# One core: the last twelve experts' weights fetched in order of use, first scan steps prepared among the convolutions, bias product behind K

## What is computed

```
u = rms_norm(h, norm_mix_g)
q, k, v, z, xbc, dt_raw, gate_logits = split(u @ w_in)
y_attn = sliding_window_attention(q, k, v, sinks, rel_bias)      # T5 bias by distance
xbc = silu(causal_depthwise_conv(xbc, conv_w, conv_b))           # 24 tiles of 128 channels
y_ssm = chunked scan over 128 positions, 4 groups of 8 heads      # 2 chunks, then gated norm
merged = gate0 * (y_attn @ w_attn_br) + gate1 * (y_ssm @ w_ssm_br)
h = h + merged @ w_out
logits = rms_norm(h) @ w_router + b_router;  top 4 of 32 experts, softmax weights
for e in range(32):  h += weight_e * ((swiglu(u @ w1[e] + b1[e])) @ w2[e] + b2[e])
out = rms_norm(h, norm_final_g)[16:]
```

## Time and profile before

| | |
|---|---|
| median of three runs | 1416.4 us |
| the profiled execution, its own time | 1421.5 us |
| its span, first to last instruction | 1419.3 us |
| PE busy, share of the span | 93% |
| DVE, ACT, POOL busy | 28%, 19%, 3% |
| chain that ended last | PE 51%, DMA 44%, ACT 2%, DVE 2% |
| DMA rate in the expert stage | 429 GB/s |
| TensorE clock, mean granted | 0.975 |

### The profile page before, as it was taken

The page is one execution under the profiler, slowest core; times in us unless marked ns, Lnnn a source line. Parts: engine busy times, 40 slices in busy tenths (PEclk is TensorE's granted clock), DMA queues, the critical chain, the costliest instruction groups (busy, mean ns, idle before and its releaser), DMA issues.

```text
span 1419.3 us, 18777 instructions
## 1 busy us (share of the span) xinstructions
PE 1315.8 (93%) x7431; PEld 677.6 (48%) x7431; DVE 391.7 (28%) x942; ACT 272.3 (19%) x629; POOL 44.0 (3%) x48
## 2 busy tenths in 40 slices
PE   9999999799999999998899989998899988999897
PEld 5677787455887534343333433333333333333332
DVE  1055466578213432121111211112111121112112
ACT  2124333456200311111111111111111111111111
POOL 3000100031000000000000000000000000000000
PEclk8999999899999999999999999999999999999999
DMA  9533433234875599999999999999999999999993
GB/s 324 155 120 107 131 122 127 104 113 129 285 252 222 208 412 429 429 429 429 429 429 429 429 429 429 429 429 429 429 429 429 429 429 429 429 429 429 429 375 161
DMA packets 73870, 468.49 MB, mean 330 GB/s; under 512 B 4867, under 2 KB 37915, under 8 KB 49228
## 3 DMA queue, kind: packets, MB, share of 16 engines
q1 hardware_dynamic: 70444, 457.89, 79.6%
q0 software_dynamic: 1952, 5.61, 1.4%
q10 hardware_dynamic: 1440, 4.52, 0.9%
HBM read 466.61 MB, written 1.13 MB: 330 GB/s over the span
## 4 chain that ended last, share of the span: by engine, by line
PE 51%; DMA 44%; ACT 2%; DVE 2%; issue 1%; POOL 0%; SPq 0%; DVEq 0%; ACTq 0%; POOLq 0%
PE bank L1271 49%; DMA ring<-in_w 43%; PE bank L1312 0%; DMA rows<-in_g_ssm 0%; PE bank L1381 0%; DVE ring L970 0%; ACT arena L728 0%; ACT arena L642 0%; PE bank L1556 0%; DVE arena L1104 0%; PE bank L1383 0%; PE bank L1665 0%; DVE arena L933 0%; ACT wdt L811 0%; PE bank L1450 0%
## 5 line engine op out<-in xcount | busy, mean ns | idle before, releaser
L1271 PE MATMUL bank<-ring,arena 128*64 128x512 f32 (+3 forms) x2296 | 577.1, 611 | 76.3 <-DMA ring<-in_w 70.3
L1271 PEld LDWEIGHTS bank<-ring,arena 128*64 128x64 f32 (+2 forms) x2296 | 202.4, 146 | 406.6 <-issue 338.7
L1271 PE MATMUL bank<-arena 128*128 128x64 bf16 (+7 forms) x3048 | 358.2, 356 | 7.8 <-ACT arena L709 4.7
L1271 PEld LDWEIGHTS bank<-arena 128*128 128x128 bf16 (+4 forms) x3048 | 177.1, 121 | 210.4 <-issue 195.4
L1271 PE MATMUL bank<-arena,ring 128*128 128x256 f32 (+2 forms) x1312 | 270.0, 386 | 2.5 <-ACT decays L634 1.6
L1271 PEld LDWEIGHTS bank<-arena,ring 128*128 128x128 f32 (+1 forms) x1312 | 217.4, 181 | 45.3 <-ACT decays L634 1.8
L1185 DVE TENSOR_SCALAR arena<-bank 128x256 f32<-128x256 f32 x64 | 27.1, 423 | 697.4 <-PE bank L1271 697.4
L816 ACT ACTIVATE arena<-arena 128x256 f32<-128x256 f32 x64 | 26.7, 417 | 395.1 <-DVE arena L1185 395.1
L823 ACT ACTIVATE arena<-bank 128x512 f32<-128x512 f32 x32 | 19.1, 597 | 310.4 <-PE bank L1271 310.4
L1271 PE MATMUL bank<-arena,wdt 64*128 64x512 f32 (+1 forms) x280 | 69.4, 602 | 0.7 <-ACT arena L823 0.7
L816 ACT ACT_TABLE_LOAD x32 | 41.1, 1283 | 0.6
(11 more groups left out here) (235 smaller groups left out, 584.6 us busy)
## 6 DMA issues: line engine op xcount, KB each, us to landing
ring<-in_w SPq DMA_DIRECT2D x128, 2048.0 KB, 25.4
arena<-in_w SPq DMA_DIRECT2D x64, 2048.0 KB, 29.2
ring<-in_w_in SPq DMA_DIRECT2D x34, 1024.0 KB, 5.4
ring<-in_w_ssm SPq DMA_DIRECT2D x8, 1024.0 KB, 7.9
arena<-cum_rows ACTq DMA_DIRECT2D x8, 512.0 KB, 4.3
ring<-in_w_att SPq DMA_DIRECT2D x16, 256.0 KB, 6.9
ring<-in_w_out SPq DMA_DIRECT2D x4, 1024.0 KB, 4.8
arena<-bias_rows POOLq DMA_DIRECT2D x1, 2048.0 KB, 11.1
```

What stands on the lines that cost most here:

```text
L1271: return tn.matmul(o, lhsT, rhs, start=first, stop=last, skip_group_check=True)
```

## The change

Four edits. (1) From expert 20 on SP issues an expert's six parts in the order in which PE uses them; at the turn, two parts of expert 21 go ahead of expert 20's parts 4 and 5. (2) `ssd_exp` of the first two steps moves to iterations 14 and 18, `ssd_cb` to 14 and 15 (both in bank 7), `ssd_pre` to 17 and 21. (3) The first states go to banks 6, 6, 1 and 5, the first z tile to bank 0, and the last group's `state0` and `st0_save` behind the first scan step. (4) The bias product moves behind the K projection, its eviction behind K's; one more warm-up product stands in each of the two places.

```
-            return bank[it % 2 if it else 3]
+            return bank[it % 2]
+        st0_bank = [bank[6], bank[6], bank[1], bank[5]]
-            return bank[4 + it % 2 if it else 7]
+            return bank[4 + it % 2 if it > 1 else 7][:, P * (it == 1):P * (it == 1) + P]
...
-            def last_two(used):
...
+            TURN = 20
+            def in_order_of_use(used):
+                half = DOUBLED.stop // 2
+                doubled(expert_sources(TURN + 1), (TURN + 1) % 2, used, range(half))
+                single(expert_sources(TURN), TURN % 2, used)
+                doubled(expert_sources(TURN + 1), (TURN + 1) % 2, used, range(half, DOUBLED.stop))
+                single(expert_sources(TURN + 1), (TURN + 1) % 2, used + PARTS)
+                for e in range(TURN + 2, E):
+                    doubled(expert_sources(e), e % 2, used + PARTS * (e - TURN - 1))
+                    single(expert_sources(e), e % 2, used + PARTS * (e - TURN))
...
@@ ACT, convolution loop and scan
+                if i in (14, 18):
+                    ssd_exp((i - 14) // 4)
-                if i in (26, 27):
-                    ssd_exp(i - 26)
-                if i - 5 >= 11 and (i - 5 - 8) % 4 == 3:
+                if i - 5 >= 11 and (i - 5 - 8) % 4 == 3 and i < 28:
                     st0_save((i - 5 - 8) // 4)
             for it in range(8):
+                if it == 0:
+                    st0_save(3)
@@ DVE, convolution loop
+                if i in (17, 21):
+                    ssd_pre((i - 17) // 4)
-            for it in range(2):
-                ssd_pre(it)
@@ PE
-            keep_busy(5)
+            keep_busy(6)
...
-            keep_busy(1)
+            keep_busy(2)
...
             for j in range(2):
                 project(T_K + j, ckv, ...)
+            bias_table()
...
-                if i == 25:
-                    ssd_cb(0)
-                if i - 5 >= 11 and (i - 5 - 8) % 4 == 3:
+                if i in (14, 15):
+                    ssd_cb(i - 14)
+                if i - 5 >= 11 and (i - 5 - 8) % 4 == 3 and i < 28:
                     state0((i - 5 - 8) // 4)
...
             for it in range(8):
                 ssd_y(it)
                 if it + 1 < 8:
+                    if it == 0:
+                        pe.wait_ge(tr_saved, 20)
+                        pe.wait_ge(st0_saved, 3)
                     if it + 2 < 8:
                         ssd_cb(it + 2)
                     z_tile(it + 1)
+                    if it == 0:
+                        state0(3)
```

More of the change, by code:

```diff
@@ L446, in first_experts, with doubled @@
                     fetch(i, sources[1][i], 1)
-            def doubled(sources, odd, used):
-                for i in DOUBLED:
+            def doubled(sources, odd, used, parts=DOUBLED):
+                for i in parts:
                     sp.wait_ge(slot_used, used + (i + 1))
@@ L465, in step @@
                 single(sources, odd, used)
-            def last_two(used):
[L469 to L472, removed]
+            TURN = 20
[8 more added lines that the diff above has]
+                    single(expert_sources(e), e % 2, used + PARTS * (e - TURN))
             first_experts()
             PAIR = 2 * PARTS
-            with sp.Fori(0, E // 2 - 2) as pair:
+            with sp.Fori(0, TURN // 2 - 1) as pair:
                 step(pair * 2 + 1, 1, pair * PAIR)
                 step(pair * 2 + 2, 0, pair * PAIR + PARTS)
-            step(E - 3, 1, (E - 4) * PARTS)
-            last_two((E - 3) * PARTS)
+            step(TURN - 1, 1, (TURN - 2) * PARTS)
+            in_order_of_use((TURN - 1) * PARTS)
             sp.wait_ge(flag_ready, 1)
@@ L485, in _ @@
                     doubled(expert_sources(0), 0, b * (E * PARTS) + (E - 2) * PARTS)
[L486 removed]
+                    with sp.Fori(0, TURN // 2) as pair:
                         step(pair * 2, 0, b * (E * PARTS) + (pair * PAIR + (E - 1) * PARTS))
                         step(pair * 2 + 1, 1, b * (E * PARTS) + (pair * PAIR + E * PARTS))
[L489 to L491 removed]
+                    in_order_of_use(b * (E * PARTS) + (E + TURN - 1) * PARTS)
                 sp.wait_ge(slot_used, PASSES * E * PARTS - PARTS + 1)
@@ L615, in _ @@
                 saved(sc.activation(kT[:, j, :], b[:, 0:NT], ACT.Copy))
+            act.wait_ge(avec_ready, 1)
+            ch.link(sc.activation(avec[0:HEADS, 0, :], bank[5][0:HEADS, 0:VL], ACT.Copy))
+            sc.activation(avec[0:HEADS, 1, :], bank[6][0:HEADS, 0:VL], ACT.Copy).then_inc(avec_saved, 1)
             act.wait_ge(pads_set, 1)
@@ L708, in st0_save @@
                 act.wait_ge(st0_ready, g + 1)
-                sc.activation(hst[:, g, :], bank[6][:, :], ACT.Copy).then_inc(st0_saved, 1)
+                sc.activation(hst[:, g, :], st0_bank[g][:, :], ACT.Copy).then_inc(st0_saved, 1)
             def z_evict(it):
@@ L993, in xdecay0 @@
                                      sc_(decays[0:META, 1, 0, 8 * g:8 * g + 8]), ALU.mult), xdec0_ready, g + 1)
[L995 to L1002, removed]
             def heads(v_, h0=0):
@@ L1019, in ssd_pre @@
                 done(v.tensor_tensor(em[:, it % 2, :, :], em[:, it % 2, :, :],
-                                     cb_bank(it)[:, 0:BLK].unsqueeze(1).to_broadcast([P, HPG, BLK]), ALU.mult), m_ready, it + 1)
+                                     cb_bank(it).unsqueeze(1).to_broadcast([P, HPG, BLK]), ALU.mult), m_ready, it + 1)
+            dve.wait_ge(decay_ready, 1)
+            for i in range(24 + 5):
+                if i < 24:
+                    conv(i)
+                if 0 <= i - 1 < 24:
+                    silu(i - 1)
+                if i - 4 >= 11 and (i - 4 - 8) % 4 == 3:
+                    xdecay0((i - 4 - 8) // 4)
+                if i in (17, 21):
+                    ssd_pre((i - 17) // 4)
             def group_scale(half):
```

26 lines of the change are left out of this document (13 added, 13 removed).

## The result

The changed kernel takes 1402.56 us, median of four runs (1400.53 to 1405.31), against 1416.2 for the kernel before in the same series (1415.23 to 1416.95). The ratio is 0.99 with a 95% interval of 0.9885 to 0.9914. So it is faster, by 13.6 us, and not by 23.6; its time lies just above the range of 1387 to 1401. The profiled execution took 1401.74 us.

A forecast was written before the change was run, and what follows sets the result against it. Weight transfer was taken to pace the experts from the fifth on, PE the end and nearly all before the experts. 10.5 + 8.2 + 4.9 = 23.6 us off gave 1392.8 for the runs, range 1387 to 1401.

The forecast's parts named there:

- Experts: Expert loads in order of use: 7.4 + 3.3 less a hole of 0 to 1.5; 10.5 us gained, range 8 to 12.
- Waits ahead of parts 2 and 3: Expert stage: PE's new waits for parts 2 and 3, put at 1.4 us each.
- a hole of about 1 at the turn: Turn to the new load order at experts 20 and 21: queue runs dry for 0 to 1.5 us.
- an end 5.6 to 7.1 behind the last landing: Last expert: PE ends 5.6 us after the last load lands, instead of 13.0.
- Scan and convolutions: Scan's start: second step 12.5 us earlier, less 4.3 of added loop work; net 8.2, range 2 to 10.5.
- The loop took on: Convolution loop: added work costs 2.0 + 1.6 + 0.5 + 0.2 = 4.3 us, from 2 to 11.
- Start: Kernel's start: with the clock held, K and the bias product end at 23.5 against 28.47; gain 4.9 us.
- I subtract the sum from both: Whole kernel: 23.6 us taken from the profiled 1421.5 and from the median of the runs, 5.1 lower.
- the transposes take 4.3 at full clock in every trace, not 2.7: Start: the 24 transposes would take about 2.7 us with the clock held.
- the idle moment of 0.88 that the sixth warm-up product was to cover: Start: PE's idle moment before the clock's fall, to be covered by a sixth warm-up product so the clock holds.
- The listed sign for being wrong: Start: a half clock in the first 20 us would show the prediction wrong.
- The clock falls at the start: Rival at the start: the clock falls despite the added wide product; 1392.8 + 6.0 = 1398.8, chance 0.2.

The follow-up runs named there:

- before-again: The kernel before, unchanged, profiled once more: 1417.22 us, ratio 1.0003; its profiled execution took 1417.01 with a span of 1414.9.
- e5: Edits 1 to 3 with the start of before, against the kernel before: 1402.13 us, ratio 0.9894.
- e9: e5 with products on constants in PE's waits at the first convolution and iterations 15 and 19: 1398.11 us, ratio 0.9874 against the kernel before.
- e10: e5 with ssd_exp moved to iterations 16 and 20 and ssd_pre to 20 and 24: 1396.04 us, ratio 0.9851 against the kernel before.
- e12: e10 with products on constants also filling the first convolution's wait: 1395.8 us, ratio 0.9858 against the kernel before.
- e2: Only the order of the expert loads from expert 20 on, on the kernel before: 1406.88 us, ratio 0.9927.
- e4: Only the start edit (bias product behind K, two more warm-up products), on the kernel before: 1420.21 us, ratio 1.0022.
- e7: The kernel before with a sixth product in the first warm-up and nothing else: 1417.8 us, ratio 1.0009.
- e3: Only the scan and convolution edits (2 and 3), the scan-only kernel, on the kernel before: 1408.69 us, ratio 0.9951.
- e6: The kernel before with the bias product and its eviction behind K, no added warm-up product: 1418.36 us, ratio 1.001.
- e8: e5 with both ssd_exp at iteration 14: 1405.93 us, ratio 0.9928 against the kernel before.
- e11: e4 with two products on constants in the wait at the first convolution: 1419.19 us, ratio 1.001 against the kernel before.

## Why the prediction was half right

**Experts: right.** 10.5 expected; 9.6 alone, and 10.1 to 10.4 in the traces between the second scan step and the end (before-again 1414.9 - 292.24, changed kernel 1399.9 - 287.37, e5, e9, e10 and e12 likewise). Only e2's own trace, the slowest of its five executions, shows less: 8.3 (1406.4 - 292.05 = 1114.4 against before-again's 1122.7). Waits ahead of parts 2 and 3, a hole of about 1 at the turn, and an end 5.6 to 7.1 behind the last landing were much as put.

**Scan and convolutions: right in sum and in mechanism.** 8.2 expected, 8.3 in the trace, 7.8 in the times. The loop took on 4.05 (4.3 expected): the first scan step of the scan-only kernel starts at 272.53, and without the loop's cost it would be 272.49 less the 4.01 by which the first trace ran late (282.87 in the earlier trace rows against 278.86 in before-again). Of it 2.55 had arisen by iteration 15 (231.08 against 228.53) and 1.49 more by iteration 19 (250.97 against 246.93); nothing came behind that. Expected were 2.0 and 1.6, and 0.7 for `ssd_pre` and the masks. The next activation started 0.01 to 0.02 us behind each of the four added table loads, and taking two of them out did not make the kernel faster. The Trainium skill ("ScalarE: Activation LUTs", What ACT_TABLE_LOAD costs) has a drain of some 1.38 us with every switch. The traces disagree. What the prediction didn't have is that these longer waits of 3.5 and 2.4 can bring the clock down, 4.3 us in the trace of e5.

**Start: wrong, and this is the step that failed.** +4.9 was expected, -3.7 measured, 8.6 of the 10 us that are missing. The step is the sentence "I subtract the sum from both". The 4.9 consisted of the half clock between 12.5 and 22.7 in the one profiled execution, whose time stood 5.1 above the other runs. That number was in the text, and was treated as an offset; it was the very loss that the term wins back. The median had never paid it. Of the other 1.4 us 0.9 are the experts' (9.6) and 0.4 the scan's (7.8). Had the start been worked out for an execution without the fall, the term would have been zero at best: a product moved behind K costs the same there, and two products are added to PE, which waits for little at that place. Smaller errors stand beside it: the transposes take 4.3 at full clock in every trace, not 2.7; and the idle moment of 0.88 that the sixth warm-up product was to cover stood behind ten warm-up passes of 6.10, while in before-again they took 7.24 and left no gap. With a sixth product the next work began 0.9 later in e4 (10.48 against 9.61), and no later in e7 (9.62). The listed sign for being wrong, a half clock in the first 20 us, did not appear; the clock held, and the gain was absent all the same.

**The rivals.** "The clock falls at the start" gave 1398.8 and did not occur: full clock, yet slower than that. The right rival would have been "the clock did not fall before, either".

**Where the 15.0 us between the traces of before-again and of the changed kernel come from:** start -1.87 (24.27 to 26.14), fall at the first convolution -1.5 (5.36 against 3.83), scan +8.3, experts +10.1. The medians differ by 13.6; two of the four runs of the changed kernel lie at 1403.4 and 1405.3, where the falls seen in e5 would put them. That was not traced, and stays open. Single executions 4 to 5 us above their median also stand in e3 (two of six), e6, e8, e9 and e12 (one each), all without the full start edit, and none among the 22 of e4 and e11, which have it; whether that edit prevents the fall of the first trace, now and then, was not tested.

## What to carry to other kernels

Before a loss in a profile is booked as an edit's gain, ask whether the profiled execution pays it and the median doesn't: where the profiled time stands above the other runs, look for the difference in the trace first, and take a second trace. A delay in a pipelined loop is priced by the next thing that needs the delayed result: the same exponentials cost 4 us ahead of the save that everybody waits for, and 1.5 to 1.8 behind it. Where a wait of a few us on TensorE can't be removed, a few products on constants in it are a cheap test, and perhaps a cure, for a clock that falls there.

## What the hardware showed unexpectedly

The clock of one and the same program falls in one execution and not in the next. Ahead of the scan both traces of the kernel before have the same wait; behind it two products took 2.08 in the first and 1.12 in the second:

```profile
275.63 2.08 PE L1271 MATMUL bank<-ring,arena 128*128 128x512 f32 x2 [2.75 <-DVE ring L992]
```

```profile
271.62 1.12 PE L1271 MATMUL bank<-ring,arena 128*128 128x512 f32 x2 [2.75 <-DVE ring L992]
```

Ahead of the first convolution, waits of 2.30 to 2.53 us were followed by full clock (seven traces, among them before-again with 2.53 and e5 with 2.32) and waits of 2.34, 2.47, 2.49 and 2.31 by half clock (changed kernel, e4, e7, e6); a wait of 3.50 at iteration 15 was followed by full clock in the changed kernel and the scan-only one, and by half in e5. The Trainium skill ("TensorE: Matmul & The Clock Gate", What's actually happening) says that the chip's look at PE's activity runs free of the program, so that the same kernel meets it in another phase each time. The traces fit that: the same warm-up's ten passes took 6.10 us in one and 7.24 in the other of the two traces of the kernel before, and the length of a wait within 2.3 to 3.5 us did not tell what followed. But the four kernels that fell at the first convolution are just the four traces with a changed start and that wait unfilled, one trace each; whether the start decides or chance does isn't shown. No wait below 1.4 us in the convolution loop was followed by half clock in any trace; at the start, half clock did come soon after an idle moment of 0.88. A fall cost 1.5 to 1.7 us behind a wait of 2.3 to 2.5, and 2.7 behind the 3.50 of e5.
